# Second attention: turning a batch's probabilities ahead of the value products of the batch before it

## The chip, the cores and the metric

The kernel runs on one core of a Trainium2 chip. The metric is the device time of one execution in microseconds; it is given as the median of the runs. TensorE does the matmuls and transposes, VectorE (DVE in the rows) the row maxima and weight splitting, ScalarE (ACT) the exponentials and most copies out of PSUM, GpSimd (POOL) some additions, and SyncE (SP) issues most transfers.

## What is computed

Two network blocks over 512 tokens of width 1024, in float32. The first is a state-space mixer with a feed-forward part. The second puts 16 meta tokens in front (528 positions in all) and runs two attention layers, each with a gated feed-forward part. The change lies in the second of these, the differential attention. Per head it builds two probability maps, subtracts one from the other and multiplies the difference with the values:

```python
def attn_map(qb, kk):
    lg = jnp.einsum('bqhd,bshd->bhqs', qb, kk).astype(jnp.float32) * scale + bias
    return jax.nn.softmax(jnp.where(mask, lg, NEG_INF), axis=-1)

a = attn_map(q1b, k1) - lam * attn_map(q2b, k2)
return jnp.einsum('bhqs,bshd->bqhd', a.astype(vb.dtype), vb)
```

There are 8 heads. Afterwards each head's output is normalised and projected with `w_o`. The mask lets a query see only its own chunk and earlier ones, so later query tiles have more keys.

## The kernel before, in words

Every engine has a program written by hand; engines wait for each other by semaphores only, and each engine runs its own instructions in the order in which they are written. There is no scheduler. The second attention takes from about 1800 to 2090 us of the span.

**Pairs and batches.** The heads are worked in four pairs, `j` = 0 to 3 (two heads of a pair are `hp` = 0, 1). The five query tiles of a pair (16 meta tokens, then four tiles of 128) make four batches `b`: tiles 0 and 1, tile 2, tile 3, tile 4. For each batch and for each of the two maps `m`:

- TensorE writes logits to PSUM (`logitsB`, L2092). Batches 0 to 2 use PSUM banks 4 and 5; batch 3 is 528 keys wide and uses banks 2 to 5.
- VectorE adds the bias and takes the row maximum (`row_maxes`, L2744, for batch 3 L2747), moving the logits out of PSUM to `probsB`. Then it negates the maxima (L2752), which raises the semaphore `B_max`.
- ScalarE exponentiates (`exps`, L1540).
- VectorE joins the two maps (`probs`, L2771), which raises `B_p`.
- TensorE turns the joined probabilities (`turn_probs`, transposes at L2113 and L2116, raises `B_tr`) into PSUM banks 2 and 3 (batch 3 also uses 4 and 5).
- ScalarE copies them to `probsTB` (`probs_out`, L1551, and L1553 for the last 16 rows of batch 3), which raises `B_pt`.
- TensorE multiplies them with the values (`heads`, L2134 and L2136, raises `B_pv`) into banks 6 and 7.
- ScalarE copies the product and sums its squares (`heads_out`, L1563 and L1567, raises `B_o`).

**TensorE's loop** (L2217 to L2233) goes over `b`. In iteration `b` it writes logits of map 0 of batch `b`; then a stretch of weight products that fills the time (`project`, L2056, 48 matmuls of the next pair's queries, keys or values; in the last pair `partB`, L2187, 24 matmuls of the output projection); in pairs 2 and 3 also the transpose of a finished head (`turn_head`, L2174); then logits of map 1; then `heads(j, b-2)`, and `turn_probs(j, b-1)`. Value products and turn of the last two batches follow after the loop, between the products of the next pair. Before the next pair's products stand the matmuls for the norm of its queries and keys (`head_squares`, L2071), which write bank 6 and so wait for `B_o` of the value products in that bank.

**ScalarE's loop** (L1637 to L1653) has a fixed order too: exponentials of map 0; copy of the products and the high part of a weight (`project_out`, ending with L429); in pairs 2 and 3 the copy of a turned head (L1582, L1594); `heads_out(j, b-2)`; exponentials of map 1; `probs_out(j, b-1)`.

**Waits inside `turn_probs`**, in the lines that decide here:

```python
pe.wait_ge(sem("B_p"), w + 1)
if b:
    pe.wait_ge(sem("B_pt"), w - 1)
...
if b == 2:
    pe.wait_ge(sem("B_max"), 8 * j + 8)
```

The last one keeps the turn of batch 2, which writes banks 2 and 3, behind VectorE's reading of batch 3's logits of map 1 from those banks. The other way round, `logitsB` of batch 3 map 0 waits for `B_pt` of batch 1: its banks must have been copied out by `probs_out(j, 1)`. In pair 2 `heads(2, b)` for `b` < 2 also waits for `oB_hi` (a turned head copied out of bank 6, L1582), and `heads(3, 0)` in pair 3 for `oB_ready` (VectorE's low part of a turned head, L2805).

Of the kernel before, what the change touches and what calls it, by code (L numbers as in the profile page):

```python
# [152 lines left out]
def two_block_program(nc, I, out):  # L153
    ctx = ExitStack()
    with ctx:
        sems = {}

        def sem(name):
            if name not in sems:
                sems[name] = ctx.enter_context(nc.semaphore(name))  # L160
            return sems[name]
# [572 lines left out]
        def expsA(n):  # L734
            return sum(4 if b == 0 else 2 for _, b in STEPS_A[:n + 1])
# [59 lines left out]
        def turn_no(j, b, hp):  # L795

            return 8 * j + 2 * b + hp
# [27 lines left out]
        def o_count(j, b, hp):  # L825

            return 10 * j + (2 * hp + 2 if b == 0 else 3 + 2 * b + hp)
# [4 lines left out]
        def pvB(i, hp):  # L832
            return PS[0:TT[i][1], 6 + hp, (i == 1) * P:(i == 1) * P + P]
# [6 lines left out]
        def var_count(j):  # L840

            return 4 + j + 2 + (j == 3)
# [836 lines left out]
        def _(pe):  # L1679
# [22 lines left out]
            for p in range(PG):  # L1702
                n = min(P, NROWS - p * P)
                b, c = (4, p * P) if p < 4 else (5, 0)
# [338 lines left out]
            def project(g):  # L2043
                l = L["qkv"]
                _, n, _ = qkv_tile(g)
                hi, lo, base = (HH, HL, NORM["n5"][1]) if n is None or n < 2 else (QHh, QHl, NORM["n6"][1])
                slot = (l.U0 + g) % 2
                b = 2 * (g % 2) if g < 4 else 0
                pe.wait_ge(sem("evacuated"), l.G0 + g + (1 if 1 <= g <= 4 else 2))
                pe.wait_ge(sem("w_split"), l.U0 + g + 3)  # L2050
                for k in range(KD):
                    if g < 4:
                        pe.wait_ge(sem("norm_ready"), KD * base + k + 1)
                    for w, x in ((whi, hi), (whi, lo), (wlo, hi)):
                        for h in range(2):
                            last = pe.matmul(PS[:, b + h, 0:TH], w[slot][:, k, :], x[:, k, h * TH:(h + 1) * TH],  # L2056
                                             start=(k == 0 and w is whi and x is hi),
                                             stop=(k == KD - 1 and w is wlo))
                last.then_inc(sem("units_done"), 1)

            def head_squares(j):

                pe.wait_ge(sem("evacuated"), L["qkv"].G0 + 6 * j + 6)
                if j:
                    pe.wait_ge(sem("B_o"), o_count(j - 1, 1, 0))
                else:
                    pe.wait_ge(sem("rstd"), RSTD["n5"])
                for q4 in range(4):
                    for n in range(4):
                        r = 8 * q4 + 2 * n  # L2070
                        last = pe.matmul(PS[0:32, 6, 0:132], sel_head[:, 31 - r:63 - r],  # L2071
                                         sqB[n][:, 132 * q4:132 * q4 + 132], start=(q4 == 0 and n == 0),
                                         stop=(q4 == 3 and n == 3))
                last.then_inc(sem("hn_sum"), 1)
# [44 lines left out]
            def heads(j, b):  # L2119
                for hp in range(2):  # L2120
                    w = turn_no(j, b, hp)
                    pe.wait_ge(sem("B_pt"), w + 1)
                    if w >= 2:
                        pe.wait_ge(sem("B_o"), o_count(*((j, b - 1) if b else (j - 1, 3)), hp))
                    if b == 2 and j < 3:
                        pe.wait_ge(sem("hn_var"), var_count(j + 1))
                    if j == 2 and b < 2:
                        pe.wait_ge(sem("oB_hi"), b + 2)
                    if j == 3 and b == 0:
                        pe.wait_ge(sem("oB_ready"), 6)  # L2130
                    for i in BATCH[b]:
                        nq = TT[i][1]
                        for t in range(i):
                            pe.matmul(pvB(i, hp), ptB[hp][:, t, 0:nq], vtok[:, t, hp, :], start=(t == 0), stop=False)  # L2134
                        rest = ptB[hp][0:META, 2 if i == 0 else i, 0:nq]
                        last = pe.matmul(pvB(i, hp), rest, vtok[0:META, i, hp, :], start=(i == 0), stop=True)  # L2136
                    last.then_inc(sem("B_pv"), 1)

            def turn_values(j):
                pe.wait_ge(sem("evacuated"), L["qkv"].G0 + 6 * j + 8)  # L2140
                pe.wait_ge(sem("hn_var"), var_count(j))
                if j:
                    pe.wait_ge(sem("B_pt"), 8 * j)
                    pe.wait_ge(sem("B_o"), 10 * j)
                for hd in range(2):
                    v = sqt if hd else rs
                    for t in range(4):
                        pe.transpose(PS[:, 2 + hd, t * P:(t + 1) * P], v[:, t * P:(t + 1) * P], ident)
                    pe.transpose(PS[0:META, 6 + hd, 0:P], v[:, 4 * P:T], ident).then_inc(sem("vB_trans"), 1)

            def turn_head(h):
                pe.wait_ge(sem("oB_v"), h + 1)
                if h == 0:
                    pe.wait_ge(sem("vB"), 6)
                elif h == 1:
                    pe.wait_ge(sem("oB_hi"), 1)
                elif h == 2:
                    pe.wait_ge(sem("B_o"), o_count(2, 0, 1))
                elif h == 3:
                    pe.wait_ge(sem("B_max"), 24)  # L2160
                elif h == 4:
                    pe.wait_ge(sem("vB"), 8)
                elif h == 5:
                    pe.wait_ge(sem("oB_ready"), 5)
                else:
                    pe.wait_ge(sem("B_pt"), 32)
                    pe.wait_ge(sem("B_o"), 40)
                for i in range(NT + 1):
                    q0, nq, _, _ = TT[i]
                    a, c0, _ = O_PARTS[0 if i < 3 else 1]  # L2170
                    dst = PS[:, o_bank(h) + a, q0 - c0:q0 - c0 + nq]
                    if h < 3:
                        dst = PS[:, 6, (i - 1) * P:i * P] if i else PS[:, 7, 0:META]
                    last = pe.transpose(dst, o_tok[0:nq, i, h, :], ident[0:nq, 0:nq])  # L2174
                last.then_inc(sem("oB_tr"), 1)

            def partB(f):
                l = L["ob1"]
                slot = (l.U0 + f) % 2
                pe.wait_ge(sem("evacuated"), l.G0 + f + 2)  # L2180
                pe.wait_ge(sem("w_split"), l.U0 + f + 3)
                if f == 0:
                    pe.wait_ge(sem("oB_ready"), 4)
                for k in range(4):
                    for w, x in ((whi, QHh), (whi, QHl), (wlo, QHh)):
                        for h in range(2):
                            last = pe.matmul(PS[:, h, 0:TH], w[slot][:, k, :], x[:, k, h * TH:(h + 1) * TH],  # L2187
                                             start=(k == 0 and w is whi and x is QHh),
                                             stop=(k == 3 and w is wlo))
                last.then_inc(sem("units_done"), 1)  # L2190
# [14 lines left out]
            for j in range(4):  # L2205
                more = j < 3
                head_squares(j)
                if not more:
                    turn_head(3)
                project(4 + 6 * j)  # L2210
                if j:
                    heads(j - 1, 2)
                    turn_probs(j - 1, 3)
                project(5 + 6 * j)
                if j:
                    heads(j - 1, 3)
                for b in range(4):  # L2217
                    logitsB(j, b, 0)
                    if more:
                        project(6 + 6 * j + b)  # L2220
                    else:
                        partB(b)
                    if j == 2 and b:
                        turn_head(b - 1)
                    if not more and b in (1, 2):
                        turn_head(3 + b)
                    logitsB(j, b, 1)
                    if b >= 2:
                        heads(j, b - 2)
                    if b:  # L2230
                        turn_probs(j, b - 1)
                    else:
                        turn_values(j)  # L2233
            partB(4)
            heads(3, 2)
            partB(5)
# [676 lines left out]
```

## Time and profile before

| | |
|---|---|
| median of 3 runs | 2499.92 us (2499.48 to 2509.1) |
| the profiled execution, time of the run | 2502.64 us |
| its span in the profile | 2500.6 us |
| TensorE busy over the span | 2396.1 us, 96% |
| VectorE, ScalarE, GpSimd busy | 55%, 43%, 16% |
| granted TensorE clock, 1800 to 2090 us | 0.95 of full speed |
| TensorE busy, 1800 to 2090 us | 267.93 of 290 us |
| ScalarE, VectorE busy, 1800 to 2090 us | 151.67 and 126.93 us |

A row of the timeline gives the start in us from the span's start, the length, the engine, the line of the kernel and the operation with its output and input; `x4` merges four instructions, and a bracket at the end gives idle time of the engine just before, with what ended it. PE is TensorE. Ends of matmuls are modelled and overlap the next start by some hundredths of a microsecond, so lengths of TensorE work are best read from start to start.

### The profile page before, as it was taken

The page shows a single profiled execution, that of the slowest core. Times are in us where ns is not written, and L with a number is a line of the kernel's source. Part 1 is how long each engine was busy: PE and PEld are TensorE (multiplying, and loading weights), DVE is VectorE, ACT ScalarE, POOL GpSimd, SP SyncE. Part 2 cuts the span into 40 slices and gives each one's busy share as a digit, 9 for nine tenths or more (in the row PEclk, how much of TensorE's full clock was granted, in tenths as well). Part 3 has the DMA queues.
Part 4 walks back from the last instruction along what each step waited for, and adds up shares of the span by engine and source line. Part 5 has one row for each costly group of instructions (what it writes and reads, how often), then busy time and mean ns, then how long its engine had stood idle before and what let it go on. Part 6 is the DMA issues. An engine that isn't in the chain of part 4 may idle for free.

```text
span 2500.6 us, 41318 instructions
## 1 busy us (share of the span) xinstructions
PE 2396.1 (96%) x15443; PEld 2139.1 (86%) x15443; DVE 1370.8 (55%) x2095; ACT 1062.9 (43%) x1910; POOL 397.1 (16%) x350
## 2 busy tenths in 40 slices
PE   6999999998999999998989999999999989999998
PEld 5778777887899899887868999999988779999987
DVE  5896777223465245457744666643344445766621
ACT  5646764333343233224444333322455554333322
POOL 0000444700410100100121211100100002211100
PEclk8999999999999999998989999999999999999999
DMA  8564433332233352332202233323422112232332
GB/s 291 167 204 103 108 77 85 92 101 83 85 97 93 97 136 86 99 109 57 52 18 64 84 92 86 90 89 91 136 59 62 44 52 85 84 92 85 89 95 92
DMA packets 409481, 238.38 MB, mean 95 GB/s; under 512 B 11434, under 2 KB 400397, under 8 KB 409381
## 3 DMA queue, kind: packets, MB, share of 16 engines
q1 hardware_dynamic: 400549, 202.25, 29.0%
q0 software_dynamic: 8224, 32.61, 3.8%
q10 hardware_dynamic: 608, 2.16, 0.2%
q8 instruction: 65, 1.06, 0.2%
q14 instruction: 35, 0.29, 0.0%
HBM read 234.54 MB, written 5.00 MB: 96 GB/s over the span
## 4 chain that ended last, share of the span: by engine, by line
PE 82%; DVE 6%; ACT 5%; issue 4%; DMA 3%; POOL 0%; SPq 0%; ACTq 0%; DVEq 0%; POOLq 0%
PE PS L508 60%; PE PS L2056 5%; PE PS L1842 3%; DMA w_raw<-in_w_in_dram 2%; ACT w_hi L429 1%; PE PS L2092 1%; PE PS L1857 1%; PE PS L2187 1%; PE PS L1801 1%; PE PS L2134 1%; DVE w_lo L435 1%; PE PS L1921 1%; PE PS L1957 1%; PE PS L2136 1%; PE PS L2071 1%
## 5 line engine op out<-in xcount | busy, mean ns | idle before, releaser
L435 DVE TENSOR_TENSOR w_lo<-w_raw,w_hi 128x1024 fp32r<-128x1024 f32 (+2 forms) x376 | 469.8, 1250 | 631.0 <-ACT w_hi L429 629.7
L508 PE MATMUL PS<-op_hi,w_hi 128*128 128x264 f32 (+3 forms) x2440 | 601.5, 310 | 16.2 <-DVE w_lo L435 13.4
L508 PE MATMUL PS<-op_lo,w_hi 128*128 128x264 f32 (+3 forms) x2440 | 599.0, 309 | 0.0
L508 PE MATMUL PS<-op_hi,w_lo 128*128 128x264 f32 (+3 forms) x2440 | 596.2, 308 | 0.0
L429 ACT ACTIVATE w_hi<-w_raw 128x1024 fp32r<-128x1024 f32 (+2 forms) x376 | 379.4, 1009 | 313.2 <-PE PS L508 261.6
L508 PEld LDWEIGHTS PS<-op_hi,w_hi 128*128 128x128 f32 x2440 | 397.6, 189 | 47.7 <-DVE w_lo L435 16.2
L508 PEld LDWEIGHTS PS<-op_hi,w_lo 128*128 128x128 f32 x2440 | 397.4, 189 | 22.6
L508 PEld LDWEIGHTS PS<-op_lo,w_hi 128*128 128x128 f32 x2440 | 397.0, 189 | 21.8 <-issue 0.5
L508 PE MATMUL PS<-ff_hi,w_lo 128*128 128x512 f32 (+1 forms) x784 | 240.3, 343 | 0.0
L508 PE MATMUL PS<-ff_hi,w_hi 128*128 128x512 f32 (+1 forms) x784 | 239.9, 342 | 0.0
L508 PE MATMUL PS<-ff_lo,w_hi 128*128 128x512 f32 (+1 forms) x784 | 239.9, 342 | 0.0
L1490 ACT ACTIVATE ff_u<-PS 128x528 f32<-128x528 f32 x88 | 54.0, 614 | 339.2 <-PE PS L508 319.0
L604 POOL TENSOR_TENSOR ff_u<-ff_u,rstd 128x528 f32<-128x528 f32 x88 | 99.9, 1136 | 421.0 <-ACT ff_u L1490 393.4
L508 PEld LDWEIGHTS PS<-ff_lo,w_hi 128*128 128x128 f32 x784 | 135.6, 188 | 17.8
L508 PEld LDWEIGHTS PS<-ff_hi,w_hi 128*128 128x128 f32 x784 | 135.6, 188 | 17.4
L508 PEld LDWEIGHTS PS<-ff_hi,w_lo 128*128 128x128 f32 x784 | 135.4, 188 | 17.4
L676 POOL TENSOR_TENSOR sumsq<-sumsq,evac 128x528 f32<-128x528 f32 (+1 forms) x28 | 39.1, 1397 | 524.1 <-ACT evac L649 524.1
L2685 DVE SCALAR_TENSOR_TENSOR ff_c<-ff_u,param_cols,ff_c 128x528 f32<-128x528 f32 x88 | 69.2, 786 | 12.6 <-DVE ff_c L2684 6.7
L2684 DVE SCALAR_TENSOR_TENSOR ff_c<-ff_u,param_cols,ff_c 128x528 f32<-128x528 f32 x88 | 67.7, 770 | 12.6 <-DVE ff_c L2682 6.7
L2682 DVE TENSOR_SCALAR ff_c<-ff_u,param_cols 128x528 f32<-128x528 f32 x88 | 51.1, 580 | 25.7 <-DVE ff_c L2693 14.6
L704 POOL TENSOR_TENSOR resid<-resid,evac 128x512 f32 x16 | 20.7, 1293 | 278.5 <-ACT evac L638 278.5
L620 DVE SCALAR_TENSOR_TENSOR ada_acc<-w_ada,small,ada_acc 128x512 f32<-128x512 f32 x81 | 60.8, 751 | 2.3
(497 smaller groups left out, 3866.2 us busy)
## 6 DMA issues: line engine op xcount, KB each, us to landing
w_raw<-in_w_up_dram SPq DMA_DIRECT2D x120, 512.0 KB, 3.8
w_raw<-in_w_in_dram SPq DMA_DIRECT2D x64, 512.0 KB, 4.1
w_raw<-in_w_down_dram SPq DMA_DIRECT2D x64, 512.0 KB, 3.8
w_ada<-in_w_ada_dram POOLq DMA_DIRECT2D x12, 2048.0 KB, 9.1
decay<-sums_scratch SPq DMA_DIRECT2D x16, 512.0 KB, 5.2
w_raw<-in_w_branch_ssd_dram SPq DMA_DIRECT2D x16, 512.0 KB, 4.0
w_raw<-in_w_in_a_dram SPq DMA_DIRECT2D x16, 512.0 KB, 3.8
w_raw<-in_w_kv_b_dram SPq DMA_DIRECT2D x16, 512.0 KB, 3.9
```

The lines of the kernel that those rows point to most:

```text
L429: act.activation(whi[slot][:, 0:ks, :], wraw[slot][:, 0:ks, :], ACT.Copy).then_inc(sem("w_hi_ready"), 1)
L435: dve.tensor_tensor(wlo[slot][:, 0:ks, :], wraw[slot][:, 0:ks, :], whi[slot][:, 0:ks, :].bitcast(F32), ALU.subtract).then_inc(sem("w_split ...
L508: last = pe.matmul(a[0:l.cols, h, 0:cn], w[slot][:, k, 0:l.cols], x[:, kk, c0:c0 + cn], start=(j == 0 and k == 0 and w is whi and x is l.h ...
L604: pool.tensor_tensor(x, x, rs[0:L[name].cols, :], ALU.mult).then_inc(sem("scaled"), 1)
L620: ins = dve.scalar_tensor_tensor(acc[:], w[:, k, :], small[:, 8 + k:9 + k], acc[:], ALU.mult, ALU.add)
L676: pool.tensor_tensor(sacc[:, c0:T], sacc[:, c0:T], et[g % 2][:, c0:T], ALU.add).then_inc(sem("sumsq_ready"), 1)
L1490: act.activation(halves(uu[par][:, 2:2 + T]), acc_view(l, par), ACT.Copy).then_inc(sem("evacuated"), 1)
L1842: last = pe.matmul(PS[0:rows, b + h, 0:TH], w[slot][:, k, 0:rows], x[:, k, h * TH:(h + 1) * TH], start=(k == 0 and w is whi and x is HH), ...
L2056: last = pe.matmul(PS[:, b + h, 0:TH], w[slot][:, k, :], x[:, k, h * TH:(h + 1) * TH], start=(k == 0 and w is whi and x is hi), stop=(k == ...
L2682: link(dve.tensor_scalar(c[:, :], u[:, 2:2 + T], w(2), pcol("conv_b_2", t + (x * 2 * NF + par * NF)), ALU.mult, ALU.add))
L2684: link(dve.scalar_tensor_tensor(c[:, :], u[:, 1:1 + T], w(1), c[:, :], ALU.mult, ALU.add))
L2685: dve.scalar_tensor_tensor(c[:, :], u[:, 0:T], w(0), c[:, :], ALU.mult, ALU.add).then_inc(sem("ff_conv"), 1)
```

## The change

On TensorE, `turn_probs(j, b - 1)` (and for `b` = 0 `turn_values`) is now written ahead of `heads(j, b - 2)`. `heads` exists only for `b` = 2 and 3, so eight places of the program change: iterations 2 and 3 of each of the four pairs. No instruction is added or removed, all waits stay attached to their steps, and the programs of the other four engines are the same row for row.

```diff
                     logitsB(j, b, 1)
-                    if b >= 2:
-                        heads(j, b - 2)
                     if b:
                         turn_probs(j, b - 1)
                     else:
                         turn_values(j)
+                    if b >= 2:
+                        heads(j, b - 2)
```

TensorE in iteration 2 of pair 0, in the kernel before: logits of batch 2 map 1 (`projB` 128x400), value products of batch 0 (`v_tokB`), turn of batch 1 (`mats` is the identity, `probsB`), then the first logits of batch 3 (128x264).

```order
L2092 MATMUL PS<-projB 128x400 x2
L2136 MATMUL PS<-v_tokB,probsTB_173 16x128
L2134 MATMUL PS<-v_tokB,probsTB_173 128x128
L2136 MATMUL PS<-v_tokB,probsTB_173 128x128
L2136 MATMUL PS<-v_tokB,probsTB_174 16x128
L2134 MATMUL PS<-v_tokB,probsTB_174 128x128
L2136 MATMUL PS<-v_tokB,probsTB_174 128x128
L2113 MATMUL PS<-mats,probsB_168 128x128 x2
L2116 MATMUL PS<-mats,probsB_168 16x128
L2113 MATMUL PS<-mats,probsB_169 128x128 x2
L2116 MATMUL PS<-mats,probsB_169 16x128
L2092 MATMUL PS<-projB 128x264 x4
```

The same place on TensorE in the changed kernel:

```order
L2092 MATMUL PS<-projB 128x400 x2
L2113 MATMUL PS<-mats,probsB_168 128x128 x2
L2116 MATMUL PS<-mats,probsB_168 16x128
L2113 MATMUL PS<-mats,probsB_169 128x128 x2
L2116 MATMUL PS<-mats,probsB_169 16x128
L2136 MATMUL PS<-v_tokB,probsTB_173 16x128
L2134 MATMUL PS<-v_tokB,probsTB_173 128x128
L2136 MATMUL PS<-v_tokB,probsTB_173 128x128
L2136 MATMUL PS<-v_tokB,probsTB_174 16x128
L2134 MATMUL PS<-v_tokB,probsTB_174 128x128
L2136 MATMUL PS<-v_tokB,probsTB_174 128x128
L2092 MATMUL PS<-projB 128x264 x4
```

The six transposes moved from behind the six value products to in front of them; what follows both is the same.

TensorE in iteration 3 of pair 0, in the kernel before, with the waits: logits of batch 3 map 1, value products of batch 1, then the first transpose of batch 2.

```order
L2092 MATMUL PS<-projB 128x264 [waits B_max]
L2092 MATMUL PS<-projB 128x264 x3
L2134 MATMUL PS<-v_tokB,probsTB_173 128x128 [waits B_o,B_pt]
L2134 MATMUL PS<-v_tokB,probsTB_173 128x128
L2136 MATMUL PS<-v_tokB,probsTB_173 128x128
L2134 MATMUL PS<-v_tokB,probsTB_174 128x128 [waits B_o,B_pt]
L2134 MATMUL PS<-v_tokB,probsTB_174 128x128
L2136 MATMUL PS<-v_tokB,probsTB_174 128x128
L2113 MATMUL PS<-mats,probsB_164 128x128 [waits B_max,B_pt,B_p]
```

The same place on TensorE in the changed kernel, down to the first value product:

```order
L2092 MATMUL PS<-projB 128x264 [waits B_max]
L2092 MATMUL PS<-projB 128x264 x3
L2113 MATMUL PS<-mats,probsB_164 128x128 [waits B_max,B_pt,B_p]
L2113 MATMUL PS<-mats,probsB_164 128x128 x2
L2116 MATMUL PS<-mats,probsB_164 16x128
L2113 MATMUL PS<-mats,probsB_165 128x128 [waits B_max,B_pt,B_p]
L2113 MATMUL PS<-mats,probsB_165 128x128 x2
L2116 MATMUL PS<-mats,probsB_165 16x128
L2134 MATMUL PS<-v_tokB,probsTB_173 128x128 [waits B_o,B_pt]
```

The transpose that waits for `B_max` now stands directly behind the logits from which that maximum is taken, and the value products stand behind the transposes.

## Rows read from the trace of the kernel before

**Rows 1.** The page: TensorE's busy time, and the chain that ended last, by engine.
```profile
PE 2396.1 (96%) x15443; PEld 2139.1 (86%) x15443; DVE 1370.8 (55%) x2095; ACT 1062.9 (43%) x1910; POOL 397.1 (16%) x350
...
PE 82%; DVE 6%; ACT 5%; issue 4%; DMA 3%; POOL 0%; SPq 0%; ACTq 0%; DVEq 0%; POOLq 0%
```

**Rows 2.** TensorE's waits, 1800 to 2090 us: total us, times, longest us.
```profile
PE PS L2092 <- ACT probsTB L1551: 9.0, 4, 2.3
...
PE PS L2136 <- ACT o_tok L1582: 1.2, 1, 1.2
PE PS L2136 <- DVE q_op_lo L2805: 1.1, 1, 1.1
...
PE PS L2134 <- ACT o_tok L1582: 1.0, 1, 1.0
```

**Rows 3.** TensorE's timeline, pair 1, iteration 2 into 3.
```profile
1905.65 0.94 PE L2092 MATMUL PS<-projB 64*128 64x400 f32 x4
...
1908.40 0.48 PE L2136 MATMUL PS<-v_tokB,probsTB 16*128 16x128 f32 x2
...
1909.42 0.27 PE L2116 MATMUL PS<-mats,probsB 128*16 128x128 f32 x1
1911.96 1.16 PE L2092 MATMUL PS<-projB 64*128 64x264 f32 x8 [2.27 <-ACT probsTB L1551]
```

**Rows 4.** ScalarE's timeline over the same stretch.
```profile
1907.78 0.27 ACT L1563 ACTIVATE o_tok<-PS 16x128 f32<-16x128 f32 x1
...
1908.92 0.27 ACT L1563 ACTIVATE o_tok<-PS 16x128 f32<-16x128 f32 x1 [0.22 <-PE PS L2136]
...
1909.76 0.61 ACT L1540 ACTIVATE probsB<-probsB,statsB 128x400 f32<-128x400 f32 x1
...
1910.98 0.84 ACT L1551 ACTIVATE probsTB<-PS 128x384 f32<-128x384 f32 x2
```

**Rows 5.** TensorE's timeline, pair 1, iteration 3.
```profile
1921.71 0.71 PE L2134 MATMUL PS<-v_tokB,probsTB 128*128 128x128 f32 x4
...
1923.83 0.55 PE L2113 MATMUL PS<-mats,probsB 128*128 128x128 f32 x3
...
1924.85 0.41 PE L2071 MATMUL PS<-evac,sel_head 128*32 128x132 f32 x2
```

**Rows 6.** VectorE's timeline over the same stretch.
```profile
1921.81 0.71 DVE L2747 CUSTOM_DVE_ANT_0 probsB<-PS,bias 128x528 f32<-128x528 f32 x1 [5.61 <-PE PS L2092]
...
1923.19 0.17 DVE L2752 TENSOR_SCALAR statsB<-statsB 128x2 f32<-128x2 f32 x1
```

**Rows 7.** ScalarE's timeline behind it, into pair 2.
```profile
1922.88 0.28 ACT L1563 ACTIVATE o_tok<-PS 128x128 f32<-128x128 f32 x1
...
1926.89 1.28 ACT L1615 ACT_TABLE_LOAD   x1
1928.99 0.32 ACT L1615 ACTIVATE head_ms<-head_ms 32x132 f32<-32x132 f32 x1 [0.82 <-DVE head_ms L2823]
```

**Rows 8.** Chain of work in order of time: start, length, what.
```profile
1845.48 2.13 PE PS L2092 x8
1847.61 7.85 PE PS L2056 x48
...
1863.40 6.05 PE PS L2056 x48
...
1913.12 7.57 PE PS L2056 x48
...
2037.42 3.12 PE PS L2187 x24
```

**Rows 9.** Stretch of one microsecond on TensorE: us, busy (instructions), granted clock, DMA.
```profile
1848.00:1849.00 1.00, 1.00 (x6) 0.50 0.00 0
```

**Rows 10.** TensorE's timeline, pair 3: turn of batch 0, then logits.
```profile
2033.84 0.18 PE L2116 MATMUL PS<-mats,probsB 16*16 16x16 f32 x1
...
2036.48 0.94 PE L2092 MATMUL PS<-projB 64*128 64x400 f32 x4 [1.61 <-DVE statsB L2752]
```

## What the change was predicted to do

> **What bounds the kernel now.** I read the page first. TensorE is busy 96% of the span and carries 82% of the chain that ended last [rows 1]. So a stop of TensorE in this stretch costs its full length, unless something behind it would have stopped TensorE anyway. Next I read TensorE's waits from 1800 to 2090 us, where the change lies [rows 2]. The largest is logits waiting for ScalarE's copy of turned probabilities: four waits, 9.0 us in all, 2.3 us the longest. There is one per pair, at the start of iteration 3, where the logits of batch 3 need banks 2 and 3 back. Three short ones belong to the same step of the code, each in front of value products: 1.2 us (pair 2, iteration 2), 1.1 us (pair 3, iteration 2) and 1.0 us (pair 2, iteration 3) [rows 2]. There the copy or splitting of a turned head comes late.
>
> Last I laid TensorE's timeline beside those of ScalarE and VectorE for pair 1, which is undisturbed by turned heads [rows 3 to 7]. The reader is to see two things. In iteration 2 ScalarE has no slack: it copies the value products of batch 0, exponentiates, copies the turned batch 1, and the logits start 0.14 us after that copy [rows 3, 4]. In iteration 3 the value products of batch 1 run exactly while VectorE takes the row maxima, and the turn finds its semaphore raised [rows 5, 6].
>
> **The change, iteration 2 (turn of batch 1 ahead of the value products of batch 0).** The logits end at 1906.59 (1905.65 and 0.94). Value products then run to 1908.88, the turn to 1909.69, that is 0.8 us for the turn, and the logits of batch 3 start at 1911.96 [rows 3]. ScalarE starts on the products of the first head at 1907.78, gets the second head's at 1908.92 after an idle time of 0.22 us, exponentiates from 1909.76 and copies the turned probabilities from 1910.98 to 1911.82 [rows 4]. That last copy is the one that could come sooner with an earlier turn. But it stands behind the products' copies and the exponentials in ScalarE's own program, and that program isn't changed. The turned probabilities simply lie ready longer. What does change is that the value products end 0.8 us later. ScalarE's idle time of 0.22 us in front of the second head shows that it works at TensorE's pace there, so its whole row moves by 0.8 us: products copied, exponentials, copy, and then the logits. In pairs 0 and 1 I take 0.8 us each: **+1.6 us**. Bounds: it can't be above 0.8 us, the length of the turn. It would be 0.6 us if the 0.22 us could be taken up.
>
> In pairs 2 and 3 the value products wait 1.2 and 1.1 us for something other than TensorE [rows 2]. The turn needs nothing from that and fits in (0.8 us), so the products start when they did before and ScalarE is released as before. The 0.8 us freed behind the products are idle in front of the logits, which still wait for the copy. Cost and gain: **0**. At the most it is 0.1 us each, should the turn delay the release.
>
> **Iteration 3 (turn of batch 2 ahead of the value products of batch 1).** The turn waits for B_max of batch 3 map 1. VectorE can start on these logits only when they are written, at 1921.81, and writes the negated maxima at 1923.19 plus 0.17, so 1923.36 [rows 6]. In the kernel before the products fill this time (they start at 1921.71) and the turn starts at 1923.83, after the semaphore [rows 5]. Now nothing is left to fill it. TensorE stands from the end of the logits to about 1923.4, and then still has the same turn and products to do. That is 1923.4 less 1921.75, **1.65 us** for each pair. In pair 2 the products themselves waited 1.0 us there for the turned head [rows 2]. That wait now lies inside the new one, which leaves 0.65 us. Sum: 3 times 1.65 and 0.65, **+5.6 us**. The lower bound is 1.6 a pair, the upper 1.7, by how fast the semaphore is seen.
>
> **Who is queued behind this wait.** On TensorE: the turn, the products, then head_squares, then the next pair's weight products. Head_squares starts at 1924.85 [rows 5]. It needs B_o of the first head, which ScalarE raises some 0.6 us after that head's products end (ScalarE's copy started at 1922.88, 1.1 us after TensorE began the products [rows 5, 7]). In the new order the turn ends at 1924.4, the first head's products at 1925.5, B_o comes at 1926.1, and the second head's products end at 1926.5. No further wait. ScalarE's row behind it moves by more, since its products come behind the turn too: from 1922.88 to 1925.5, 2.6 us. It loads a table at 1926.89 for 1.28 us and then has 0.82 us of idle time before the square root at 1928.99 [rows 7]. Head_squares moves the square root by 1.65 us, so there is 1.65 and 0.82 to take up 2.6 us: ScalarE is late by 0.2 us. VectorE has the last probabilities of the pair to join in the meantime, and TensorE has 6 us of weight products ahead of it [rows 8]. I count it at nothing; if it weren't covered it would cost 0.2 us in each of three pairs, 0.6 us. The queue of SyncE is not touched, apart from the rows of head_ms, which leave later by as much as TensorE is late.
>
> **Sum.** 1.6 and 5.6 are 7.2 us. No instruction is added. Against its own time, the profiled execution would go from a span of 2500.6 to 2507.8 us; its run took 2502.64 us, 2.04 around the span, so 2509.8 us. That execution lies 2.7 us above the median of 2499.92. On the median the forecast is **2507.1 us**, 0.29% more. A measurement of this kernel tells about 0.5%, 12.5 us, from no change, so this forecast lies within it, on the slow side.
>
> **TensorE's clock.** Behind a 2.3 us wait, weight products ran slow: 48 of them took 7.85 and 7.57 us in iteration 3 of pairs 0 and 1, against 6.05 elsewhere, and eight logits ahead of the first took 2.13 against 1.16 us [rows 3, 8]. The granted clock there was 0.50, the lower level of 1.2 GHz [rows 9]. One slow stretch so costs 1.5 to 2.8 us, and the kernel before has about four, one behind each wait of this kind. These waits get longer by 0.8 us, which changes nothing where the clock has fallen already. The new wait of iteration 3 is new ground. The nearest row is in pair 3: a turn from 2033.84, then 1.61 us of idle time to 2036.48, in all 2.6 us [rows 10], and the 24 products behind it took 3.12 us, 0.13 each, as fast as the 6.05 for 48 [rows 8]. The new wait has the same two parts in the other order, 1.65 and 1.0 us, so I forecast full speed.
>
> The Trainium skill, "TensorE: Matmul & The Clock Gate", Part 4, says that transposes don't count as TensorE being busy in the way that matmuls do. By that rule the wait and the turn would be one quiet stretch of 2.7 us, longer than each part, and rival A's times would be the likelier ones. The trace has its one case of such a stretch in [rows 10], and it speaks against a fall of the clock at this length.
>
> **The rivals.**
>
> *A: the clock falls in iteration 3.* The wait of 1.65 us and the small transposes and products behind it (3.1 us) give a thin stretch of 4.8 us after which head_squares and 48 weight products stand. For it: in pair 0 and 1 a thin stretch of products, turn and a 2.3 us wait did it. Against it: [rows 10]. Price: 1.5 to 2.8 us for each place, 6.0 to 11.2 us if it happens in all four, so 2513.1 to 2518.3 us. At two places it is 3 to 5.6 us, 2510 to 2513. It passes 0.5% only from three places on, or from two dear ones.
>
> *B: not slower, by the clock at iteration 3's start.* The four slow stretches of the kernel before cost 1.5 to 2.8 us each, 6 to 11 us in all. The longer wait in front of them could hold the whole of the slow time, so that logits and products behind it run at full speed. That would give back 6 to 11 against the 7.2 lost: 2496 to 2501 us. It decides from about 7 us on, that is if at least three of four disappear. Against it: in pair 0 the slow stretch reaches from the logits far into the products (2.13 and 7.85 us) [rows 8], so that 0.8 us more of waiting can't hold it.
>
> *C: the value products hide it.* If B_max came at once, or ScalarE took up the 0.8 us, only part of the sum would be left. Should iteration 2 cost nothing: 5.6 us, 2505.5. Should iteration 3 cost nothing, because TensorE would be stopped behind it anyway: 1.6 us, 2501.5. Head_squares started without a wait in [rows 5], which speaks against it.
>
> *D: the change does nothing.* TensorE executes in the order written and the order shows eight places moved, so a time equal to before could only come from C.
>
> **How the numbers follow.** Forecast, waits only and at most one fall of the clock: 2505 to 2510, chance 0.70. A at two places or more: 0.17, of which 0.12 lies beyond 0.5%. B: 0.04, of which 0.01 is faster by over 0.5%. C and D: 0.09. The predicted time is 2507.1. The range must leave out no more than 0.2: from 2502, which cuts off B, D and the largest part of C (0.10), to 2514, which cuts off the upper half of A (0.08). The median of three runs before had one run 9 us higher, so its own spread argues for no narrower range. Faster by over 0.5%: 0.01. Within 0.5%: 0.87. Slower by over 0.5%: 0.12.
>
> **What would show each step right or wrong.** In the changed kernel's profile: the wait of logits for the copy of turned probabilities goes from four times 2.3 to four times 3.0 to 3.2 us; a new wait of transposes (L2113) for VectorE's L2752 appears four times, 1.6 us each; the waits for the turned heads of 1.2 and 1.1 us shrink to 0.4 and 0.3, and that of 1.0 us goes. The logits of batch 3 in pair 1 start 0.8 us later relative to the logits before them, in pair 3 not at all later. Head_squares starts without a wait. I am wrong in iteration 2 if ScalarE's copies of the products start as early as before; in iteration 3 if the transposes find B_max raised; on the clock if 48 products behind head_squares take more than 6.1 us; and on all of it if the next pair's first logits come less than 2.4 us late in pair 1.

## The result

| | before | changed |
|---|---|---|
| median of 20 runs | 2502.11 us (2498.35 to 2509.2) | 2509.43 us (2501.73 to 2517.59) |
| ratio, changed to before | | 1.0027, 95% interval 1.0019 to 1.0035 |
| profiled execution, run and span | 2502.64 and 2500.6 us | 2507.44 and 2505.5 us |

The changed kernel is slower by 0.27%, which is 6.8 us of 2502 (4.8 to 8.8 by the interval). The forecast was 7.2 us, from a median of 2499.92 us of three runs to 2507.1; the median of 20 runs before is 2502.11, and the changed kernel's is 2509.43.

TensorE's waits from 1800 to 2100 us in the changed kernel, with the columns of [rows 2]:

```profile
PE PS L2092 <- ACT probsTB L1551: 12.3, 4, 3.1
PE PS L2113 <- DVE statsB L2752: 6.9, 4, 1.7
PE PS L2092 <- issue: 3.1, 1, 3.1
...
PE PS L2136 <- ACT o_tok L1582: 0.4, 1, 0.4
PE PS L2136 <- DVE q_op_lo L2805: 0.3, 1, 0.3
```

Against [rows 2] the wait for the copied probabilities grew from 9.0 to 12.3 us. The second row is new. The third is idle time in front of the first pair that the profile puts down to no wait; it was 2.5 us before. Two waits for turned heads shrank from 1.2 and 1.1 us to 0.4 and 0.3, and the one of 1.0 us is gone. Together that is 3.3 and 6.9, less 0.8, 0.8 and 1.0, so 7.6 us.

TensorE's timeline of pair 1 in the changed kernel, iteration 2 and then iteration 3, to be held against [rows 3, 5]:

```profile
1904.46 0.94 PE L2092 MATMUL PS<-projB 64*128 64x400 f32 x4
...
1905.94 0.27 PE L2116 MATMUL PS<-mats,probsB 128*16 128x128 f32 x1
...
1908.03 0.48 PE L2136 MATMUL PS<-v_tokB,probsTB 16*128 16x128 f32 x2
1911.59 2.13 PE L2092 MATMUL PS<-projB 64*128 64x264 f32 x8 [3.07 <-ACT probsTB L1551]
1921.15 1.16 PE L2092 MATMUL PS<-projB 64*128 64x264 f32 x8
1924.04 0.52 PE L2113 MATMUL PS<-mats,probsB 128*128 128x128 f32 x3 [1.73 <-DVE statsB L2752]
...
1926.95 0.64 PE L2071 MATMUL PS<-evac,sel_head 128*32 128x132 f32 x4
```

From the start of the logits (1905.65 and 1904.46) to the start of batch 3's logits it took 6.31 us before and 7.13 now. The difference is the length of the turn, 0.8 us. The transposes wait 1.73 us behind the logits, and head_squares follows the value products without a wait.

ScalarE's timeline of the same pair, held against [rows 4, 7]:

```profile
1907.40 0.27 ACT L1563 ACTIVATE o_tok<-PS 16x128 f32<-16x128 f32 x1 [0.77 <-PE PS L2136]
...
1909.38 0.61 ACT L1540 ACTIVATE probsB<-probsB,statsB 128x400 f32<-128x400 f32 x1
...
1910.61 0.84 ACT L1551 ACTIVATE probsTB<-PS 128x384 f32<-128x384 f32 x2
...
1926.00 0.28 ACT L1563 ACTIVATE o_tok<-PS 128x128 f32<-128x128 f32 x1 [2.69 <-PE PS L2136]
...
1930.01 1.28 ACT L1615 ACT_TABLE_LOAD   x1
1931.30 0.31 ACT L1615 ACTIVATE head_ms<-head_ms 32x132 f32<-32x132 f32 x1
```

ScalarE now stands 0.77 us for the value products, where before it found them ready. The probabilities had been turned at 1906.2, and it copied them at 1910.61, because two other steps stand ahead in its own program. The copy has a second condition: it writes the one buffer per head that the value products of batch 0 read, so it waits for them too (`B_pv`). They ended at 1908.5, and so didn't hold this copy.

VectorE's timeline of the same pair, held against [rows 6]:

```profile
1923.72 0.17 DVE L2752 TENSOR_SCALAR statsB<-statsB 128x2 f32<-128x2 f32 x1
...
1931.42 1.45 DVE L2771 SCALAR_TENSOR_TENSOR probsB<-probsB,statsB,probsB 128x528 f32<-128x528 f32 x2
1932.78 0.96 DVE L2828 RECIPROCAL head_ms<-head_ms 32x132 f32<-32x132 f32 x1
```

The new wait ends 0.15 us after VectorE has the negated maxima (1923.89 and 1924.04).

Pieces of the chain in order of time in the changed kernel (start, length, what), held against [rows 8]:

```profile
1842.90 2.13 PE PS L2092 x8
1845.04 7.70 PE PS L2056 x48
...
1862.25 6.07 PE PS L2056 x48
...
1913.72 7.50 PE PS L2056 x48
...
2040.62 4.30 PE PS L2187 x24
```

Products behind the waits of iteration 2 run slow as before, those behind the new waits of iteration 3 (1862.25) at full speed. The granted clock in pair 1 was 1.00 when the wait for the copy began, 0.55 at 1910 and 0.50 from 1911 to 1916. The last row is the place of [rows 10], which the change doesn't touch. There the kernel before took 3.12 us.

### The profile page after: what moved, and what is told of

Same layout as the page of the kernel before. It is cut to its first block, busy times and chain, and to the rows that moved or that the text cites. A ratio compares the mean times of both kernels' runs of the same rounds, so it can differ in the third digit from the quotient of the medians.

```text
span 2505.5 us, 41318 instructions
## 1 busy us (share of the span) xinstructions
PE 2390.7 (95%) x15443; PEld 2136.0 (85%) x15443; DVE 1372.9 (55%) x2095; ACT 1060.4 (42%) x1910; POOL 397.9 (16%) x350
## 4 chain that ended last, share of the span: by engine, by line
PE 82%; DVE 6%; ACT 5%; issue 4%; DMA 3%; POOL 0%; SPq 0%; ACTq 0%; DVEq 0%; POOLq 0%
PE PS L508 60%; PE PS L2056 6%; PE PS L1842 3%; DMA w_raw<-in_w_in_dram 2%; PE PS L2092 1%; PE PS L2187 1%; ACT w_hi L429 1%; PE PS L1857 1%; PE PS L1801 1%; PE PS L2134 1%; PE PS L1921 1%; DVE w_lo L435 1%; PE PS L1957 1%; PE PS L2136 1%; PE PS L2071 1%
```

## The experiments

All ratios are to the kernel before, run beside it on the same chip. They are not the quotients of the two medians; the two differ by up to 0.0013, as much as the ratio's interval reaches to one side. The theory is the prediction's: iteration 2 costs by ScalarE's order, iteration 3 by a bare wait for VectorE, and the clock stays out of it.

**Only iteration 2 swapped.**

```diff
-                    if b >= 2:
-                        heads(j, b - 2)
+                    if b == 3:
+                        heads(j, 1)
                     if b:
                         turn_probs(j, b - 1)
                     else:
                         turn_values(j)
+                    if b == 2:
+                        heads(j, 0)
```

> Only iteration 2 of each pair is swapped (turn of batch 1 ahead of the value products of batch 0); iteration 3 is as before. Theory (ScalarE's fixed order makes the late value products cost their delay, where they don't wait anyway): the wait of the logits for the copied probabilities is 3.1 us in all four pairs, but the span of pairs 0 and 1 grows by 0.8 us each and that of pairs 2 and 3 by nothing: +1.6 us in all, ratio 1.0006. No new wait of transposes. Rival (the whole difference of the changed kernel is chance of the clock or lies elsewhere): nothing measurable and no longer wait. Rival (longer waits make the clock fall further): +4 us or more.

Measured: ratio 0.9998 (0.9988 to 1.0008), medians 2502.33 and 2502.47 us. TensorE's waits in the second attention:

```profile
PE PS L2092 <- ACT probsTB L1551: 12.3, 4, 3.1
...
PE PS L2134 <- ACT o_tok L1582: 1.0, 1, 1.0
...
PE PS L2136 <- ACT o_tok L1582: 0.4, 1, 0.4
PE PS L2136 <- DVE q_op_lo L2807: 0.3, 1, 0.3
```

The waits are those of the theory: 3.3 more, 1.6 less. A cost of 1.6 us (1.0006) lies within the interval, a cost of 4 us (1.0016) does not. No cost at all lies within it too, so here the trace alone shows the 1.6 us.

**Only iteration 3 swapped** (the same edit with the two conditions exchanged).

> Only iteration 3 of each pair is swapped (turn of batch 2 ahead of the value products of batch 1). Theory: a new wait of the transposes for VectorE's negated maxima, 1.7 us four times; the 1.0 us wait of pair 2's value products goes; +5.6 to 5.9 us, ratio 1.0023. Logits of batch 3 wait 2.3 us for the copy, as before. Rival (iteration 2 carries the cost): no change in time. Rival (clock falls in iteration 3): +8 us and more, with 48 products behind head_squares above 6.1 us.

Measured: ratio 1.0032 (1.0020 to 1.0043), medians 2511.71 and 2502.47 us. TensorE's waits:

```profile
PE PS L2092 <- ACT probsTB L1551: 8.3, 4, 2.3
PE PS L2113 <- DVE statsB L2754: 6.9, 4, 1.7
```

The wait of the transposes came four times at 1.7 us, and the 1.0 us wait of pair 2 went. That is 5.9 us of the 8.0 that the ratio gives (5.0 to 10.8). The wait for the copy should have stayed at 9.0 us. In pair 2 the clock had fallen before it began: value products and turn took longer, the wait was 1.60 us, and the way from the weight products to these logits was 0.5 us longer than before. This run alone carries as much time as the whole change, so most of the cost sits in iteration 3.

**Half of the cover left in front.** In iteration 3 the value products of the first head stay ahead of the turn, those of the second stand behind it.

```diff
-                        heads(j, b - 2)
+                        heads(j, b - 2, (0, 1) if b == 2 else (0,))
                     if b:
                         turn_probs(j, b - 1)
                     else:
                         turn_values(j)
+                    if b == 3:
+                        heads(j, 1, (1,))
```

> As the kernel before, but in iteration 3 the value products of the second head stand behind the turn, those of the first head in front of it. Theory (the value products are the cover of the 1.7 us in which VectorE takes the maxima, by their length): half of the cover, 1.05 us, stays, so the transposes wait 0.6 us in pairs 0, 1 and 3 and not in pair 2: +1.8 us, ratio 1.0007. Rival (any change of order there costs the full wait, for example by the switch between transposes and products): +5.6 us as in the run with iteration 3 alone. Rival (there is slack behind): nothing.

Measured: ratio 1.0007 (0.9993 to 1.0021), medians 2505.01 and 2502.47 us. The row of TensorE's waits:

```profile
PE PS L2113 <- DVE statsB L2754: 2.0, 3, 0.7
```

Three waits of 0.7 us instead of four of 1.7, and none in pair 2. The products cover the wait by their length, about 1.05 us for one head. The interval of the time, -1.8 to 5.3 us, leaves out the 5.6 us of the rival only just and doesn't tell 1.8 us from nothing; the trace decides here.

**ScalarE copies the turned probabilities first.** TensorE as in the kernel before; in ScalarE's iteration 2 the copies of the value products go behind.

```diff
-                    if b >= 2:
+                    if b == 3:
                         heads_out(j, b - 2)
                     exps(j, b, 1)
                     if b:
                         probs_out(j, b - 1)
                     else:
                         values_out(j)
+                    if b == 2:
+                        heads_out(j, b - 2)
```

> TensorE as in the kernel before. On ScalarE, in iteration 2 only, the copies of the value products (L1563, L1567) stand behind the exponentials and the copy of the turned probabilities. Theory (ScalarE's order, not TensorE's, holds up the logits of batch 3): exponentials start at once after the weight's high part, the copy as soon as the turn is done, and the wait of the logits falls from 2.3 to 0.6 to 0.8 us in each pair: -6 to -7 us, and up to 8 us more if the clock no longer falls behind the shorter wait; ratio 0.9975 to 0.994. Rival (the wait is bound by the turn or by VectorE): the wait stays at 2.3 us and so does the time. Rival (B_o comes too late for what follows): the gain is given back as a new wait of value products in iteration 3.

Measured: ratio 0.9950 (0.9938 to 0.9962), medians 2491.82 and 2502.47 us. TensorE's waits, and ScalarE's and TensorE's timelines at the place of [rows 3, 4]:

```profile
PE PS L2094 <- ACT probsTB L1551: 2.8, 4, 0.7
```

```profile
1907.94 0.87 ACT L1551 ACTIVATE probsTB<-PS 128x384 f32<-128x384 f32 x2
```

```profile
1908.96 2.13 PE L2094 MATMUL PS<-projB 64*128 64x264 f32 x8 [0.73 <-ACT probsTB L1551]
```

The four waits of 9.0 us became 2.8. So ScalarE's order held up these logits, and TensorE's did not. The copy now starts when the turn is done; in this kernel the turn is what comes last. No new wait of value products came. The time fell by 12.5 us (9.5 to 15.5), twice the 6.2 us of waits. In pair 0 of the trace the clock stayed up as well (1.16 and 6.05 us in place of 2.13 and 7.85, 2.8 us less), in the other pairs it fell as before; where the rest went this trace doesn't show.

**The change with the same order on ScalarE.** The edit of the run before, made in the changed kernel:

```diff
-                    if b >= 2:
+                    if b == 3:
                         heads_out(j, b - 2)
                     exps(j, b, 1)
                     if b:
                         probs_out(j, b - 1)
...
+                    if b == 2:
+                        heads_out(j, b - 2)
```

> The changed kernel with ScalarE's order of the run that had the copy first: in iteration 2 the copies of the value products stand behind the exponentials and the copy of the turned batch 1. There is one buffer for turned probabilities per head, so this copy still waits for the value products of batch 0. Theory: wait of the logits 0.6 to 0.7 us in all four pairs, new wait of transposes 1.7 us four times as in the changed kernel: -1.6, -1.6, -2.4, -2.4 and +5.6, in all -2 to -3 us against the kernel before, minus what the clock gives back (0 to 6 us). Rival (iteration 3's wait is worth nothing once iteration 2 is shorter): as the run with the copy first alone, ratio 0.995.

Measured: ratio 0.9964 (0.9951 to 0.9978), medians 2496.46 and 2502.98 us. TensorE's waits:

```profile
PE PS L2115 <- DVE statsB L2754: 6.9, 4, 1.7
...
PE PS L2094 <- ACT probsTB L1551: 3.1, 4, 0.9
```

Waits went as expected, except that one of the four was 0.9 us. By the ratio the kernel is 9 us below the one before, at the end of the expected span (by the medians 6.5 us). The rival said 0.995, as without the swap; 0.9964 is above it, but the intervals overlap, so the time doesn't decide. The trace does. Iteration 3's wait is there in full, four times 1.7 us, and nothing behind it makes it up: in pair 1, from the logits behind the copy to head_squares, TensorE takes 14.56 us (1914.08 to 1928.64), and 12.98 us in the run before (1908.96 to 1921.94), with products as long (6.64 and 6.62 us).

**Work in the wait.** The changed kernel, with 22 products of 248 columns between the value products of batch 0 and the logits of batch 3 in pairs 0 to 2. They write a part of bank 1 that nobody reads.

```diff
                     if b >= 2:
                         heads(j, b - 2)
+                    if b == 2 and more:
+                        filler(j)
...
+            def filler(j):
+                pe.wait_ge(sem("evacuated"), L["qkv"].G0 + 6 * j + 8 + 3)
+                for n in range(22):
+                    pe.matmul(PS[:, 1, 264:512], QHh[:, n % 8, 0:P], QHh[:, n % 8, 0:248], start=True, stop=True)
```

> The changed kernel with 22 more products on TensorE, of 248 columns, into an unused part of a PSUM bank, in the wait in front of the logits of batch 3, in pairs 0 to 2; their results are used by nobody. They take 2.6 us, the wait is 3.1 us. Theory (the clock falls because TensorE stands still there): logits and 48 products behind them run at full speed in pairs 0 to 2 (1.1 and 6.1 us instead of 2.1 and 6.6 to 7.7), pair 3 stays slow; -5 to -8 us against the changed kernel, so about the time of the kernel before. Rival (the clock falls by the thin stretch of small products and transposes, or at a beat of its own): still slow in at least two pairs and no gain. Rival (the filler runs over the end of the wait): +1 us per pair.

Measured: ratio 1.0001 (0.9988 to 1.0013), medians 2502.47 and 2502.98 us. That is 0.0026 below the changed kernel, 6.5 us, by added work. The two were each measured against their own runs of the kernel before; their intervals don't meet. TensorE's timeline of pair 1, and pieces of its chain in pairs 1 and 2:

```profile
1903.51 2.80 PE L2142 MATMUL PS<-q_op_hi 128*128 128x248 f32 x22
1906.65 1.16 PE L2092 MATMUL PS<-projB 64*128 64x264 f32 x8 [0.34 <-ACT probsTB L1551]
```

```profile
1907.81 6.04 PE PS L2056 x48
...
1971.56 4.31 PE PS L2142 x22
1975.86 1.09 PE PS L2092 x8
1976.95 6.05 PE PS L2056 x48
```

In pairs 0 to 2 logits and products behind the wait ran at full speed (1.1 and 6.05 us), and pair 3, without filler, stayed slow (2.13 and 4.20 us). In pair 1 the changed kernel's granted clock fell to 0.55 at 1910, in the wait; here it was 1.00 all through. So in pairs 0 and 1 the fall came with TensorE standing still, as the theory says. In pair 2 the filler itself took 4.31 us: the granted clock was 1.00 until 1972, then 0.55 and 0.50, the lower level. There it fell half a microsecond into the filler, behind 3.5 us of transposes and value products in which TensorE stood still for no more than 0.37 us. For this pair the first rival was right about the fall, though not about what follows, since the clock was back for the logits. The second rival was right there too: the filler ran over the end of the wait, and from the end of the weight products the logits came 1.2 us later than in the changed kernel (9.39 and 8.16 us).

**A second buffer, with and without the swap.** The turned probabilities of batch 0 go to tiles that are free in this layer, so ScalarE needn't wait for batch 0's value products before it copies batch 1's. The edit's lines on ScalarE for iteration 2, in which it copies first:

```diff
+                    if b == 2:
+                        probs_out(j, 1)
+                        exps(j, 2, 1)
+                        heads_out(j, 0)
+                        continue
```

One kernel has TensorE's iteration 2 swapped as in the first experiment, the other has TensorE's order of before. Iteration 3 is as before in both.

> Swap in iteration 2 only (turn of batch 1 ahead of the value products of batch 0), a second buffer for the turned batch 0 (in tiles that are free in this layer, one small copy more per head), and on ScalarE in iteration 2 first the copy of the turned batch 1, then the exponentials, then the copies of the value products. Theory (the turn's earlier place is worth what its consumer makes of it): the copy ends while TensorE multiplies, so the logits of batch 3 don't wait at all: -2.3 us in each pair, and -0.8 in each of pairs 2 and 3 where the turn fills the wait for the turned head, together -10 to -11 us, and up to 8 us more from the clock; ratio 0.993 to 0.996. Rival (the exponentials behind the copy become late and VectorE's joining in iteration 3 waits): part of it comes back as waits of VectorE and then of transposes in iteration 3.

> The same second buffer and ScalarE order as in the run with two buffers and the swap, but TensorE's order as in the kernel before. Theory: the copy must wait for the turn, which ends last on TensorE, so the logits wait 0.6 to 0.9 us in each pair: about the time of the run with the copy first alone (ratio 0.995), 4 to 5 us above the run with the swap. Rival (the buffer alone does it): no wait of the logits here either, same time as with the swap.

Measured: with the swap, ratio 0.9917 (0.9903 to 0.9930), median 2481.63 us; without it, 0.9949 (0.9936 to 0.9963), 2493.55 us; before 2502.98 us. Pair 1 with the swap, TensorE and then ScalarE:

```profile
1897.09 0.27 PE L2128 MATMUL PS<-mats,probsB 128*16 128x128 f32 x1
...
1899.18 0.48 PE L2152 MATMUL PS<-v_tokB,sumsq 16*128 16x128 f32 x2
1899.60 1.16 PE L2104 MATMUL PS<-projB 64*128 64x264 f32 x8
```

```profile
1896.72 1.06 ACT L429 ACTIVATE w_hi<-w_raw 128x1024 fp32r<-128x1024 f32 x1
1897.67 0.87 ACT L1558 ACTIVATE probsTB<-PS 128x384 f32<-128x384 f32 x2
1898.41 0.65 ACT L1540 ACTIVATE probsB<-probsB,statsB 128x400 f32<-128x400 f32 x1
```

Without the swap, the row of TensorE's waits reads:

```profile
PE PS L2104 <- ACT probsTB L1558: 2.8, 4, 0.7
```

With the swap this row is gone. The turn ends at 1897.4, the copy runs from 1897.67 to 1898.54 while TensorE multiplies, and the logits of batch 3 follow the value products without a wait. No transposes waited in iteration 3, where the rival had expected it. Without the swap the second buffer, and the copy ahead of the exponentials, change nothing that can be measured against the run with the copy first (0.9949 and 0.9950). The swap of iteration 2 that only lengthens waits in the changed kernel is worth 0.0032 here, 8 us (11.9 by the medians; the intervals of the two ratios don't meet). The trace shows 10.6 us of waits gone against the kernel before (9.0, and 0.8 in each of pairs 2 and 3) and full speed behind them in pairs 0 and 1; in pairs 2 and 3 the clock fell as before. The measured 21 us (17.5 to 24.3) are more than I expected, and the two traces don't hold all of them: from the second stretch of 48 products to the first feed-forward product it took 274.1 us before and 259.4 here, 14.7 less. The part in front of that, the same in both kernels, was 6.6 us longer in the trace of before.

## Why the prediction was right

**Iteration 2.** Forecast 0.8 us each in pairs 0 and 1 and nothing in pairs 2 and 3; by waits 3.3 less 1.6, so 1.7 us in place of 1.6. The lengths say the same: from the end of the weight products to the logits of batch 3, pair 0 went from 6.25 to 7.05 us and pair 1 grew by 0.8, while pairs 2 and 3 stayed (8.17 and 8.16, 8.14 and 8.14). The reason held too: ScalarE copied in its own order. The run with the copy first and the pair of runs with two buffers show it from both sides.

**Iteration 3.** Forecast 1.65 us a pair and 0.65 in pair 2, in all 5.6; measured 6.9 less 1.0, so 5.9 us. The wait was 1.73 us. I had put 0.05 us between the maxima and the first transpose, and it was 0.15. Read from start to start, from the logits of batch 3's map 1 to the next weight products, the iteration grew by 1.58, 1.57, 0.57 and 1.75 us in the four pairs, 5.5 in all. The next pair's first logits came 3.3 us late in pair 1 against the logits of iteration 2; 0.9 of that is the clock behind the copy's wait, and 2.4 is what I had named. The run with iteration 3 alone gave 0.32% (0.20 to 0.43), and half of the cover left three waits of 0.7 us.

**What was counted at nothing.** Head_squares started without a wait. ScalarE's square root was late by 0.2 us as worked out: its table load ended at 1931.29 and the root came at once, while VectorE had written head_ms at 1931.05. VectorE joined the last probabilities until 1932.87 and took the reciprocal then, so the 0.2 us were covered.

**The clock.** Rival A did not happen: in the four traces with iteration 3 fully swapped (the changed kernel, iteration 3 alone, the change with the copy first, the filler) none of the sixteen places ran slow. But the row on which I rested this was weaker than I took it for. The place of [rows 10] took 3.12 us for 24 products in the kernel before, and 4.30 in the changed kernel, where nothing about it is changed. In the ten traces of this case it took 3.12 to 3.15 us seven times and 3.99 to 4.51 three times. One row of one execution shows that a stretch of 2.6 us can pass at full speed, not that it will. Nor does a fall in iteration 3 need the new wait: in two traces with the old order there (only iteration 2 swapped, two buffers without the swap) head_squares of pair 2 took 4.71 and 4.61 us instead of 3.73, with a granted clock down to 0.50. That A stayed away was forecast on thin grounds, and luck had a part in it. The Trainium skill's rule that transposes don't count as TensorE being busy in the same way ("TensorE: Matmul & The Clock Gate", Part 4) is neither shown nor refuted by these rows.

**Rival B** was wrong as put (a longer wait doesn't hold the slow time: 2.13 and 7.70 us in pair 0 as against 2.13 and 7.85). Its price was right. The slow stretches in iteration 3 cost 2.6, 2.4 and 1.6 us in pairs 0 to 2, by logits and products of the changed kernel against those of the filler (9.83, 9.63 and 8.72 us against 7.20, 7.20 and 7.14), where the price was 1.5 to 2.8.

**The profiled executions** differ by 4.9 us in span. From the second stretch of 48 products to the first feed-forward product the changed kernel takes 285.4 us against 274.1, so 11.3 more. Of that 7.6 are the waits above and 0.6 the wait marked "issue". The rest, about 3 us, fits the clock in places that the change doesn't touch: 48 products at the start of pair 0 took 7.55 us and not 6.05, and 24 in pair 3 the 4.30 above. In front of it, the changed kernel's execution was 5.5 us faster by chance. Medians of many runs weigh the change; a pair of spans doesn't.

## What to carry to other kernels

Moving a step earlier on one engine is worth what the engine that consumes it makes of it. Look at the consumer's own order, and at the buffer into which it writes, before the producer's is changed: here the same swap of iteration 2 added 1.7 us of waits under one order of ScalarE and gained 0.3% under another with a second buffer. And a step that seems only to be in the way may be the cover of a wait behind it: when a step with a semaphore moves ahead of work without one, its wait shows, up to the length of the work that it passed (1.7 us for 2.1 us of value products, 0.7 us for half of them).

## What the runs showed of the hardware

- Useless products in a wait of 3.1 us made the kernel faster by 0.26% (two ratios, 1.0001 and 1.0027, each to the kernel before). The products behind the wait ran wholly at the upper level of the clock, 2.4 GHz, instead of starting at 1.2 GHz (6.05 us for 48 instead of 6.6 to 7.7).
- The clock can fall without a long wait. In pair 2 of the kernel with the filler it fell to 0.55 and 0.50 at 1972, behind 3.5 us of transposes and value products with one wait of 0.37 us, and the filler took 4.31 us instead of 2.80.
- At one place where TensorE's order is the same in all ten kernels ([rows 10]), the clock fell in three traces and not in the other seven (24 products in 3.99 to 4.51 and in 3.12 to 3.15 us). Fifteen runs of the kernel before went from 2493.7 us, with a mean granted clock of 0.981, to 2506.9 us with 0.975.
